# A two-block transformer step on one core: output projection, second norm and first queries ahead of the expert layer, in another order

## The chip, the cores and the metric

The kernel runs on one NeuronCore of a Trainium2 chip. The metric is the device time of one execution in microseconds, as the median of several runs; lower is better. PE (TensorE), ACT (ScalarE), DVE (VectorE) and POOL (GpSimd) each work through a queue of their own in a fixed order; SP issues the loads of weights and tables. Engines meet at semaphores only.

## The reference, cut to what matters

Two blocks are run one after the other. The first has two layers on 256 tokens `h` and 256 context tokens `hc`, width 1024; at the end of each layer:

```python
h = h + mod[:, 2] * mix                                   # mix = merged @ w_out
xn2 = modulate(rms_norm(h, norm2_g[l]), mod[:, 3], mod[:, 4])
h = h + mod[:, 5] * peer_ffn(xn2, peer_wq[l], peer_keys[l], peer_u[l], peer_v[l])
# peer_ffn, for each chunk of 128 tokens: q = xc @ w_q (8 heads x 2 halves x 128); scores of each half
# against 128 keys; the best 16 of each, the best 16 of their sums, softmax -> gates; for each of the
# 8 * 16 experts chosen: gelu(u_e . x) * gate * v_e, summed
```

All arithmetic is in float32. The second block (two layers of feed-forward, mixer and feed-forward) isn't touched by the change.

## The kernel before

Tokens are tiled in blocks of 128: blocks 0 and 1 are the tokens, 2 and 3 the context. The work is written out as one program for each engine (`tensor`, `scalar`, `vector`, `gpsimd`, `sync`, from line 2411 on), built of stages; each stage has a part for PE, ACT and DVE (`pe_...`, `act_...`, `dve_...`).

The expert layer is the long part. For each block 128 gathers run (one for each head and choice: 8 heads x 16), each of 1 MB: for each token the u and the v row of its expert (`pool_gather`, L2567), into a ring of up to ten slots. DVE forms u . x (L1718), ACT the gelu's tanh (L1147) and a diagonal of weights (L1132), and PE adds v through that diagonal (L699), which gives the slot back to POOL. The order of the gathers is fixed: stage A (layer 0) takes blocks 0, 1, 2, 3, stage C (layer 1) blocks 0, 1. `weave` puts other work between the steps of an expert stage in a fixed order: in A the routing of the other heads and blocks, the context's mixer and the next layer's start, in C the other heads' queries (`pe_rest`) and block 1's routing.

Routing turns queries into expert numbers, for two heads at a time (a head group): scores of the queries against the keys (PE, L675), copied by ACT (L1112), the best 16 and their pairs by DVE (`dve_route_pass`, L1609 to L1686), with an exponential by ACT (L1120). Block 0's first head group yields the indices of the first 32 gathers.

Ahead of each of the two expert stages stands a stretch with little beside it, written for both blocks at once. For T = "A" and T = "C" it runs:

- `pe_mixer_end`: the merged rows of both blocks are turned (L423; copied back by ACT L1075 and DVE L1574), then for each half n of the output columns the gate's rows (L423, copied by ACT L1081) and the product with w_out for both blocks (L430). DVE multiplies by the gate and adds to H (L1586, L1588), ACT takes the square sum (L921). A product of `gemm8` over 512 columns shows in the profile as 16 passes of 512 columns.
- the second norm, `pe_norm_turn`: one chain for both blocks (L1349, L1340, root L926, L1353), a diagonal for each block (L1359), then H is turned and scaled by PE (L456), with gain and shift by ACT (L939) and DVE (L1375), one half each.
- `pe_peer_rows`: the normed rows turned back for the experts (L423; copies L1095 and L1597).
- `pe_queries`: head group 0's queries, four products of eight matmuls over 256 columns, both blocks' tokens (L430; copies L1104 and L1606), which show as 64 passes.
- `pe_route_scores`: scores of block 0, group 0, followed by its routing.

`fence` makes ACT and DVE wait for all three engines; `edge` only marks how far each has come, for a later `after_edge`. Fences stand behind the mixer ("mixed A"), behind the attention of C ("attended D"), behind `mixer_end` ("ended") and behind the norm ("gather"); POOL starts the gathers after the mark "gather", and SP loads the keys after "ended A" and "attended D". SP's queue is in order: output weights (`("out", T, n)`), keys, then the query weights (`("wq", T, n)`, two loads of 1 MB for each head group) through a ring of four slots of 1 MB; a load waits until the slot's last reader is done.

## Time and profile before

| | us |
|---|---|
| median of 3 runs (4346.28 to 4356.92) | 4348.15 |
| profiled execution, first to last instruction (its own time: no other figure is given for it) | 4350.1 |
| PE busy | 3741.8 (86%) |
| DVE busy | 2841.1 (65%) |
| ACT busy | 1154.3 (27%) |
| POOL busy | 898.6 (21%) |
| first gather of stage A | 649.98 |
| first gather of stage C | 2575.40 |

The profile is that of one execution; times count from its first instruction. A matmul in float32 shows as two passes for each instruction. "L430" is line 430 of the kernel; an arrow in brackets names what ended the idle time in front of a row. PEld is the load of weights into PE, which lies beside the matmuls.

### The profile page before, as it was taken

What the parts mean: (1) busy time and instruction counts of PE and PEld (TensorE: products, weight loads), DVE (VectorE), ACT (ScalarE), POOL (GpSimd) and SP (SyncE); (2) the same over time, 40 slices, a digit from 0 to 9 for tenths busy, and PEclk for the clock granted to TensorE, in tenths of its full rate; (3) what the DMA queues carried; (4) which work ended last, traced back from release to release, by engine and by line L of the source; (5) the groups of instructions that cost most, each with busy time, mean ns of one, the idle gap of its engine ahead of it and who ended that gap; (6) DMA issues with size and microseconds to landing.
All of it is one profiled execution on the core that took longest, in us unless ns stands there. A gap on an engine that the chain in (4) does not pass through costs nothing. (4 is left out here: it accounts for less than half of the span.)

```text
span 4350.1 us, 42327 instructions
## 1 busy us (share of the span) xinstructions
PE 3741.8 (86%) x15261; PEld 2387.3 (55%) x15261; DVE 2841.1 (65%) x6605; ACT 1154.3 (27%) x2555; POOL 898.6 (21%) x772
## 2 busy tenths in 40 slices
PE   7999987878999867689896778777779989999898
PEld 3457554334755523245642545222229879898797
DVE  1342137897877788977876548886656576565765
ACT  2141011124111111231011411111124444444443
POOL 0000003433332334423331014543320000000000
PEclk7999998999999999999997889999999999999999
DMA  7273439998999999989996159999984534545443
GB/s 296 78 271 119 163 141 356 386 368 303 394 420 379 390 361 403 389 307 389 421 421 254 68 203 387 421 383 422 421 356 161 179 132 171 186 158 184 136 165 131
DMA packets 246623, 1225.90 MB, mean 282 GB/s; under 512 B 19257, under 2 KB 46203, under 8 KB 124429
## 3 DMA queue, kind: packets, MB, share of 16 engines
q0 software_dynamic: 110592, 805.36, 45.7%
q1 hardware_dynamic: 135820, 417.84, 26.0%
q8 instruction: 120, 1.97, 0.2%
q14 instruction: 91, 0.74, 0.0%
HBM read 1222.07 MB, written 1.05 MB: 281 GB/s over the span
## 5 line engine op out<-in xcount | busy, mean ns | idle before, releaser
L430 PE MATMUL ps<-wbuf,BIG 128*128 128x512 f32 x1856 | 813.3, 595 | 6.9 <-DMA wbuf<-in_t_conv_out_w 2.8
L2567 POOL DMA_INDIRECT gbuf<-in_t_uv,idx x286 | 341.3, 1193 | 1508.2 <-DVE BIG L1683 882.4
L430 PEld LDWEIGHTS ps<-wbuf,BIG 128*128 128x128 f32 x1856 | 352.7, 191 | 441.4 <-issue 433.3
L1759 DVE TENSOR_TENSOR plo<-wbuf,phi 128x1024 fp32r<-128x1024 f32 (+1 forms) x344 | 401.6, 1180 | 284.4 <-ACT phi L1167 283.7
L699 PE MATMUL ps<-gbuf,BIG 128*128 128x512 f32 x868 | 435.4, 641 | 165.8 <-ACT BIG L1132 165.4
L699 PE MATMUL ps<-BIG 128*128 128x512 f32 x904 | 438.2, 625 | 116.2 <-ACT BIG L1132 110.6
L1147 ACT ACTIVATE BIG<-BIG 128x2 f32<-128x2 f32 x384 | 78.1, 203 | 1430.9 <-DVE BIG L1725 1419.8
L724 PE MATMUL ps<-XH,phi 128*128 128x256 f32 x1472 | 422.0, 287 | 24.7 <-DVE XL L1769 20.8
L1718 DVE CUSTOM_DVE_ANT_0 BIG<-BIG 128x1024 f32<-128x1024 f32 x292 | 355.8, 1221 | 121.8 <-DMA BIG<-in_t_uv,idx 121.0
L430 PE MATMUL ps<-BIG,wbuf 128*128 128x256 f32 x1920 | 421.9, 380 | 0.3 <-DMA wbuf<-in_t_conv 0.2
L2567 POOL DMA_INDIRECT BIG<-in_t_uv,idx x292 | 337.6, 1156 | 406.5 <-PE ps L699 341.8
L1167 ACT CAST phi<-wbuf 128x1024 fp32r<-128x1024 f32 (+1 forms) x344 | 343.8, 1013 | 289.6 <-PE ps L726 289.1
L726 PE MATMUL ps<-XH,plo 128*128 128x256 f32 x1472 | 420.5, 286 | 0.0
L725 PE MATMUL ps<-XL,phi 128*128 128x256 f32 x1472 | 420.5, 286 | 0.0
L1718 DVE CUSTOM_DVE_ANT_0 gbuf<-gbuf,BIG 128x1024 f32<-128x1024 f32 x286 | 348.6, 1221 | 109.0 <-DMA gbuf<-in_t_uv,idx 108.6
L430 PEld LDWEIGHTS ps<-BIG,wbuf 128*128 128x128 f32 x1920 | 365.4, 191 | 64.7 <-issue 14.1
L699 PEld LDWEIGHTS ps<-gbuf,BIG 128*128 128x128 f32 x868 | 166.2, 202 | 409.6 <-ACT BIG L1132 231.5
L699 PE MATMUL ps<-wbuf,BIG 128*128 128x512 f32 x604 | 300.4, 627 | 94.2 <-ACT BIG L1132 94.0
L699 PEld LDWEIGHTS ps<-BIG 128*128 128x128 f32 x904 | 172.4, 198 | 363.6 <-issue 191.6
L2567 POOL DMA_INDIRECT wbuf<-in_t_uv,idx x190 | 219.5, 1155 | 417.0 <-PE ps L699 389.8
L724 PEld LDWEIGHTS ps<-XH,phi 128*128 128x128 f32 x1472 | 286.6, 195 | 26.7 <-DVE XL L1769 22.2
L1132 ACT ACTIVATE BIG<-ident,BIG 128x128 f32<-128x128 f32 x594 | 210.3, 395 | 298.3 <-DVE BIG L1701 276.8
(348 smaller groups left out, 5079.6 us busy)
## 6 DMA issues: line engine op xcount, KB each, us to landing
wbuf<-in_t_in SPq DMA_DIRECT2D x84, 1024.0 KB
wbuf<-in_t_w_mod SPq DMA_DIRECT2D x48, 1024.0 KB
wbuf<-in_ffn_wg SPq DMA_DIRECT2D x20, 2048.0 KB, 7.8
wbuf<-in_ffn_wu SPq DMA_DIRECT2D x20, 2048.0 KB, 7.8
wbuf<-in_t_conv SPq DMA_DIRECT2D x48, 768.0 KB
wbuf<-in_ffn_wd SPq DMA_DIRECT2D x16, 2048.0 KB, 8.0
wbuf<-in_t_peer_wq SPq DMA_DIRECT2D x24, 1024.0 KB
wbuf<-in_w_in SPq DMA_DIRECT2D x14, 1536.0 KB, 6.6
```

Source lines behind the costliest of these rows:

```text
L430: ins = p(mm)(bank, l, r, start=(k == 0), stop=(k == 7))
L699: ins = p(mm)(ps.of(("acc", T, tb, n)), dg, g[:, 1024 + n * 512:1536 + n * 512], start=(j == 0), stop=(j == last_on_pe(T, tb)))
L724: p(mm)(bank, lh, rh, start=(start and i == 0), stop=False)
L725: p(mm)(bank, lh, rl, start=False, stop=False)
L726: ins = p(mm)(bank, ll, rh, start=False, stop=(stop and i == n - 1))
L1132: a(act)(dg, ident[:, :], ACT.Copy, scale=wv[:, j:j + 1]).then_inc(act_exp.up(T, tb, "diag", j), 1)
L1147: a(act)(x2[:, j - 1:j + 1], x2[:, j - 1:j + 1], ACT.Tanh, scale=GELU_C * GELU_K).then_inc(act_exp.up(T, tb, "tanh", j // 2), 1)
L1167: a(copy)(piece_at(q)[0], W2.of(key, rows_, n)[:, k0:k1, c0:c1]).then_inc(act_piece.up(q), 1)
L1718: v(ttr)(row, row, XN[:, tb, :], 1.0, 0.0, ALU.mult, ALU.add, hid[:, j:j + 1]).then_inc(dve_exp.up(T, tb, "u", j), 1)
L1759: v(tt)(lo, W2.of(key, rows_, n)[:, k0:k1, c0:c1], hi.bitcast(F32), ALU.subtract).then_inc(dve_piece.up(q), 1)
L2567: g(nc.gpsimd.indirect_dma_start)(slot, None, I["t_uv"], bass.IndirectOffsetOnAxis(ap=idx[:, tb % 3, j:j + 1], axis=0)).then_inc(g_landed[ ...
```

## The change

For T = "A" and T = "C", the stages between the mixer (or attention) and the experts are replaced by one function for each engine, which takes the blocks one behind the other:

- PE's order is: block 0 turned, gate 0, product (n 0, block 0), gate 1, block 1 turned, products (1, 0) and (0, 1), norm of block 0, product (1, 1), rows of block 0, queries of block 0 (128 columns), its scores, then norm, rows and queries of block 1.
- The second norm has a chain for each block, so every instruction of that chain on DVE and ACT is issued twice, on one column in place of two. Queries are 128 passes of 128 columns in place of 64 of 256, with a copy for each block and product (eight in place of four).
- Block 0's halves are copied by ACT alone where the merged rows are turned; block 1's normed half, rows and queries are copied by ACT alone.
- The fences "ended" and "gather" become marks, in C also "attended D"; "mixed A" stays a fence.
- SP loads the keys behind the query weights of head group 0 instead of ahead of them; in A the mark "ended A" stands behind product (1, 1) and its square sum.
- Block 0's route pass on ACT copies the scores, does block 1's norm, rows and queries, and then its exponential.
- Context blocks ("B") are as before.

```diff
+        def pe_to_experts(p, T, l, L):
+            XT, MM = L.XT, L.MM
+            def merged_turn(tb):
+                for half in range(2):
+                    b = ps.claim(p, ("mt", T, tb, half), ((act_proj, dve_proj)[half * tb], (T, "mt", tb, half)))
+                    p.wait_ge(*(dve_att.at(T, tb, "merged") if T == "C" else dve_mix.at(T, "m", 1, 2, tb)))
+                    turn4(p, b, [MM[:, tb, k * 128:(k + 1) * 128] for k in range(half * 4, half * 4 + 4)]).then_inc(
+                        pe_proj.up(T, "mt", tb, half), 1)
+            def gate(n):
+                pe_gate_rows(p, ("og", T, n), l, 2, n, 0, act_proj, T, "gate", n).then_inc(pe_proj.up(T, "gate", n), 1)
+            def product(n, tb):
+                b = ps.claim(p, ("op", T, n, tb), (dve_proj, (T, "m", n, tb)))
+                p.wait_ge(*act_proj.at(T, "mt", tb, 0))
+                p.wait_ge(*(act_proj, dve_proj)[tb].at(T, "mt", tb, 1))
+                gemm8(p, b, ("out", T, n), 512, lambda k, w: (XT[:, k, tb * 128:(tb + 1) * 128], w)).then_inc(
+                    pe_proj.up(T, "op", n, tb), 1)
+                halves_done(("out", T, n), pe_proj, T, "op", n, tb)
+            def normed(tb):
+                N = second_norm(T, tb)
+                for half in range(2):
+                    b = ps.claim(p, ("norm", N, tb, half), ((act_norm, dve_norm)[half * (1 - tb)], (N, tb, "x")))
+                    p.wait_ge(*dve_norm.at(N, tb, "diag"))
+                    dg = diag_of(N, tb)
+                    for j in range(4):
+                        k = half * 4 + j
+                        ins = p(mm)(b[:, j * 128:(j + 1) * 128], H[:, tb, k * 128:(k + 1) * 128], dg, start=True, stop=True)
+                    ins.then_inc(pe_norm.up(N, tb, half), 1)
+            def rows_turned(tb):
+                N = second_norm(T, tb)
+                p.wait_ge(*act_norm.at(N, tb, "x"))
+                if tb == 0:
+                    p.wait_ge(*dve_norm.at(N, tb, "x"))
+                for half in range(2):
+                    b = ps.claim(p, ("xn", T, tb, half), ((act_peer, dve_peer)[half * (1 - tb)], (T, "xn", tb, half)))
+                    turn4(p, b, [XT[:, k, tb * 128:(tb + 1) * 128] for k in range(half * 4, half * 4 + 4)]).then_inc(
+                        pe_peer.up(T, "xn", tb, half), 1)
+            def queries(tb):
+                for j in range(4):
+                    b = ps.claim(p, ("pq", T, 0, j, tb), ((act_peer, dve_peer)[j % 2 * (1 - tb)], (T, "pq", 0, j, tb)))
+                    gemm8(p, b[:, 0:128], ("wq", T, 0), 512,
+                          lambda k, w: (w[:, j * 128:(j + 1) * 128], XT[:, k, tb * 128:(tb + 1) * 128])).then_inc(
+                              pe_peer.up(T, "pq", 0, j, tb), 1)
+                halves_done(("wq", T, 0), pe_peer, T, "pq", 0, 3, tb)
+            merged_turn(0)
+            gate(0)
+            product(0, 0)
+            gate(1)
+            merged_turn(1)
+            product(1, 0)
+            product(0, 1)
+            normed(0)
+            product(1, 1)
+            edge(p, "ended " + T)
+            rows_turned(0)
+            queries(0)
+            run(pe_route_scores(p, T, T, 0, 0, 2))
+            normed(1)
+            edge(p, "gather " + T)
+            rows_turned(1)
+            queries(1)
...
+        def act_to_experts(a, T, l, L):
+            XT = L.XT
+            def merged_turn(tb):
+                for half in range(2 - tb):
+                    a.wait_ge(*pe_proj.at(T, "mt", tb, half))
+                    a(copy)(XT[:, half * 4:half * 4 + 4, tb * 128:(tb + 1) * 128],
+                      ps.of(("mt", T, tb, half)).rearrange("p (j t) -> p j t", j=4)).then_inc(
+                          act_proj.up(T, "mt", tb, half), 1)
+            def gate(n):
+                g = tmp.enter(a, ("og", T, n))
+                a.wait_ge(*pe_proj.at(T, "gate", n))
+                a(copy)(g, ps.of(("og", T, n))).then_inc(act_proj.up(T, "gate", n), 1)
+            def squares(n, tb):
+                a.wait_ge(*dve_proj.at(T, "h", n, tb))
+                act_square_sum(a, T, tb, n, tmp.of(("om", T, n, tb)), norm_before(T))
+            def normed(tb):
+                N, scale, shift = second_norm(T, tb), colA(l, 1), colB(l, 1)
+                for half in range(1 + tb):
+                    b = ps.of(("norm", N, tb, half))
+                    a.wait_ge(*pe_norm.at(N, tb, half))
+                    for j in range(4):
+                        ins = a(act)(xt(L, half * 4 + j, tb), b[:, j * 128:(j + 1) * 128],
+                                ACT.Identity, bias=shift(half * 4 + j, tb), scale=scale(half * 4 + j, tb))
+                ins.then_inc(act_norm.up(N, tb, "x"), 1)
+            def rooted(tb):
+                N = second_norm(T, tb)
+                act_root(a, norm_row(N, (tb,)), dve_norm.at(N, "mean"), act_norm, N, "root")
+            def rows_copied(tb):
+                for half in range(1 + tb):
+                    a.wait_ge(*pe_peer.at(T, "xn", tb, half))
+                    a(copy)(XN[:, tb, half * 512:(half + 1) * 512], ps.of(("xn", T, tb, half))).then_inc(
+                        act_peer.up(T, "xn", tb, half), 1)
+            def queries(tb):
+                for j in range(0, 4, 2 - tb):
+                    a.wait_ge(*pe_peer.at(T, "pq", 0, j, tb))
+                    a(copy)(PQ[:, j, tb * 128:(tb + 1) * 128], ps.of(("pq", T, 0, j, tb))[:, 0:128]).then_inc(
+                        act_peer.up(T, "pq", 0, j, tb), 1)
+            merged_turn(0)
+            gate(0)
+            gate(1)
+            squares(0, 0)
+            merged_turn(1)
+            squares(1, 0)
+            rooted(0)
+            normed(0)
+            squares(0, 1)
+            squares(1, 1)
+            edge(a, "ended " + T)
+            rows_copied(0)
+            rooted(1)
+            queries(0)
+            route = act_route_pass(a, T, 0, route_before(T, 0, 0), 0, 2)
+            next(route)
+            normed(1)
+            edge(a, "gather " + T)
+            rows_copied(1)
+            queries(1)
+            run(route)
...
+        def dve_to_experts(v, T, l, L):
+            XT = L.XT
+            def summed(n, tb):
+                nn, g = slice(n * 512, (n + 1) * 512), tmp.of(("og", T, n))
+                m = tmp.claim(v, ("om", T, n, tb), (act_square, (T, tb, n)))
+                v.wait_ge(*pe_proj.at(T, "op", n, tb))
+                v.wait_ge(*act_proj.at(T, "gate", n))
+                v(tt)(m, ps.of(("op", T, n, tb)), g, ALU.mult).then_inc(dve_proj.up(T, "m", n, tb), 1)
+                v.wait_ge(*dve_proj.now())
+                v(tt)(H[:, tb, nn], H[:, tb, nn], m, ALU.add).then_inc(dve_proj.up(T, "h", n, tb), 1)
+            def norm_diagonal(tb):
+                N = second_norm(T, tb)
+                r = sts.claim(v, ("nm", N), (dve_norm, (N, tb, "diag")))[:, 0:1]
+                for n in range(2):
+                    v.wait_ge(*act_square.at(T, tb, n))
+                v(tt)(r, ssq[:, tb:tb + 1, 0], ssq[:, tb:tb + 1, 1], ALU.add).then_inc(dve_norm.up(N, "sum"), 1)
+                v.wait_ge(*dve_norm.now())
+                dve_mean(v, r, r, D, dve_norm, N, "mean")
+                v.wait_ge(*act_norm.at(N, "root"))
+                v(recip)(r, r).then_inc(dve_norm.up(), 1)
+                s = big.claim(v, ("dg", N, tb), (pe_norm, (N, tb, 1)))
+                v.wait_ge(*dve_norm.now())
+                v(ts)(s[:, 0:128], ident[:, :], r, None, ALU.mult).then_inc(dve_norm.up(N, tb, "diag"), 1)
+            for n in range(2):
+                tmp.take(("og", T, n), (dve_proj, (T, "m", n, 1)))
+            summed(0, 0)
+            v.wait_ge(*pe_proj.at(T, "mt", 1, 1))
+            v(vcopy)(XT[:, 4:8, 128:256], ps.of(("mt", T, 1, 1)).rearrange("p (j t) -> p j t", j=4)).then_inc(
+                dve_proj.up(T, "mt", 1, 1), 1)
+            summed(1, 0)
+            norm_diagonal(0)
+            summed(0, 1)
+            N, scale, shift = second_norm(T, 0), colA(l, 1), colB(l, 1)
+            v.wait_ge(*pe_norm.at(N, 0, 1))
+            for j in range(4):
+                ins = v(ts)(xt(L, 4 + j, 0), ps.of(("norm", N, 0, 1))[:, j * 128:(j + 1) * 128],
+                            scale(4 + j, 0), shift(4 + j, 0), ALU.mult, ALU.add)
+            ins.then_inc(dve_norm.up(N, 0, "x"), 1)
+            summed(1, 1)
+            edge(v, "ended " + T)
+            v.wait_ge(*pe_peer.at(T, "xn", 0, 1))
+            v(vcopy)(XN[:, 0, 512:1024], ps.of(("xn", T, 0, 1))).then_inc(dve_peer.up(T, "xn", 0, 1), 1)
+            norm_diagonal(1)
+            edge(v, "gather " + T)
+            for j in (1, 3):
+                v.wait_ge(*pe_peer.at(T, "pq", 0, j, 0))
+                v(vcopy)(PQ[:, j, 0:128], ps.of(("pq", T, 0, j, 0))[:, 0:128]).then_inc(dve_peer.up(T, "pq", 0, j, 0), 1)
+            run(dve_route_pass(v, T, l, 0, 0, 2))
...
-        def queries_in(p, T, K, n):
-            split = n == 0 and T != "B"
-            p.wait_ge(*act_peer.at(T, "pq", n, 2 if split else 3))
-            if split:
-                p.wait_ge(*dve_peer.at(T, "pq", n, 3))
+        def queries_in(p, T, K, tb, n):
+            if n or T == "B":
+                p.wait_ge(*act_peer.at(T, "pq", n, 3))
+            elif tb:
+                p.wait_ge(*act_peer.at(T, "pq", 0, 3, 1))
+            else:
+                p.wait_ge(*act_peer.at(T, "pq", 0, 2, 0))
...
-            run(pe_mixer_end(p, "A", 0, first))
-            edge(p, "ended A")
-            run(pe_norm_turn(p, "A2", range(2)))
-            edge(p, "gather A")
-            run(pe_peer_rows(p, "A", "A2", 0, first.XT, 0, 1))
-            run(pe_queries(p, "A", first.XT, range(1), 1))
-            run(pe_route_scores(p, "A", "A", 0, 0, 2))
+            pe_to_experts(p, "A", 0, first)
             weave(pe_experts(p, 0, AB, 0, 256), pe_context(p), 2)
...
-            fence(a, "attended D")
-            run(act_mixer_end(a, "C", 1, second, tmp))
-            fence(a, "ended C")
-            run(act_norm_turn(a, "C2", second, range(2), colA(1, 1), colB(1, 1)))
-            fence(a, "gather C")
-            run(act_peer_rows(a, "C", 0, 1))
-            run(act_queries(a, "C", range(1), 1))
-            run(act_route_pass(a, "C", 0, route_before("C", 0, 0), 0, 2))
+            edge(a, "attended D")
+            act_to_experts(a, "C", 1, second)
...
-            fence(v, "attended D")
+            edge(v, "attended D")
             tmp.reset()
-            run(dve_mixer_end(v, "C", 1, second, tmp))
-            fence(v, "ended C")
             big.reset()
-            run(dve_norm_turn(v, "C2", second, range(2), colA(1, 1), colB(1, 1), "C", big))
-            fence(v, "gather C")
-            run(dve_peer_rows(v, "C", 0, 1))
-            run(dve_queries(v, "C", range(1), 1))
-            run(dve_route_pass(v, "C", 1, 0, 0, 2))
+            dve_to_experts(v, "C", 1, second)
             weave(dve_experts(v, C, 0, 128), both(dve_rest(v, "C", 1), scaled(dve_route_pass(v, "C", 1, 1), 1.0, 1)), 2, BEHIND)
...
         def sync_peer(s, T, l):
-            if T != "B":
-                after_edge(s, {"A": "ended A", "C": "attended D"}[T])
-                load(s, ("keys", T), KY, I["t_keys"][l].rearrange("p (c k) -> p c k", c=16))
             for n in range(4):
                 two_halves(s, ("wq", T, n), I["t_peer_wq"][l, n])
+                if n == 0 and T != "B":
+                    after_edge(s, {"A": "ended A", "C": "attended D"}[T])
+                    load(s, ("keys", T), KY, I["t_keys"][l].rearrange("p (c k) -> p c k", c=16))
 ```

The call sites of ACT and DVE in A, and of PE in C, are changed in the same way.

## Rows read from the trace of the kernel before

**Rows 1.** Chain that ended last, 2530 to 2600: start us, us, what

```profile
2540.05 13.83 PE ps L430 x64
...
2554.59 1.14 PE ps L675 x8
...
2575.40 0.94 POOL gbuf L2567
```

**Rows 2.** Timeline, 565 to 650: start us, us, engine, line, operation, tiles, count, [idle before <-releaser]

```profile
569.95 0.69 DVE L1564 TENSOR_TENSOR BIG<-BIG,gbuf 128x512 f32<-128x512 f32 x1
...
570.81 1.17 ACT L1075 COPY BIG<-ps 128x512 f32<-128x512 f32 x2 [14.79 <-DVE BIG L1564]
...
572.78 13.97 PE L430 MATMUL ps<-wbuf,BIG 128*128 128x512 f32 x32 [0.55 <-DVE BIG L1574]
...
586.59 0.60 PE L423 MATMUL ps<-ident,modd 128*128 128x128 f32 x4
...
587.02 13.90 PE L430 MATMUL ps<-wbuf,BIG 128*128 128x512 f32 x32
...
602.41 0.63 ACT L921 ACTIVATE gbuf<-H 128x512 f32<-128x512 f32 x1 [6.14 <-DVE H L1588]
...
603.16 0.16 DVE L1349 TENSOR_TENSOR st<-ssq 128x2 f32<-128x2 f32 x1 [0.79 <-ACT gbuf L921]
...
603.63 1.28 ACT L926 ACT_TABLE_LOAD   x1 [0.50 <-DVE st L1340]
...
605.77 6.10 PE L456 MATMUL ps<-gbuf,H 128*128 128x128 f32 x32 [4.85 <-DVE gbuf L1359]
607.88 1.50 ACT L939 ACTIVATE BIG<-ps,modd,modA 128x128 f32<-128x128 f32 x4 [2.76 <-PE ps L456]
...
611.71 1.04 PE L423 MATMUL ps<-ident,BIG 128*128 128x128 f32 x8
...
614.32 13.98 PE L430 MATMUL ps<-BIG,wbuf 128*128 128x256 f32 x64
...
629.02 1.13 PE L675 MATMUL ps<-BIG 128*128 128x128 f32 x8 [0.72 <-DVE BIG L1606]
629.88 11.10 PEld L430 LDWEIGHTS ps<-BIG,wbuf 128*128 128x128 f32 x52
...
649.17 0.23 ACT L1120 ACTIVATE BIG<-BIG 128x32 f32<-128x32 f32 x1 [17.10 <-DVE BIG L1676]
...
649.98 1.08 POOL L2567 DMA_INDIRECT gbuf<-in_t_uv,idx  x1 [649.53 <-DVE BIG L1683]
```

**Rows 3.** Windows: us; busy us of each engine; TensorE clock granted, DMA share, GB/s

```profile
2486.00:2496.20 10.20, 2.65 (x25) 2.42 (x23) 6.49 (x7) 3.65 (x6) 0.00 (x0) 0.76 0.01 2
2498.90:2501.60 2.70, 2.70 (x4) 1.17 (x4) 0.00 (x0) 0.59 (x1) 0.00 (x0) 0.51 0.55 231
2522.00:2528.00 6.00, 6.00 (x15) 2.47 (x13) 0.95 (x2) 0.72 (x2) 0.00 (x0) 1.00 0.00 0
2590.00:2620.00 30.00, 24.78 (x57) 10.90 (x57) 27.86 (x100) 5.28 (x17) 12.18 (x12) 0.94 1.02 422
```

**Rows 4.** Timeline, 2482 to 2500

```profile
2487.61 1.04 PE L423 MATMUL ps<-ident,BIG 128*128 128x128 f32 x8
...
2490.66 0.21 ACT L926 ACTIVATE st<-st 128x8 f32<-128x8 f32 x1 [0.19 <-DVE st L1340]
...
2496.20 1.97 PE L423 MATMUL ps<-ident,BIG 128*128 128x128 f32 x8 [7.54 <-DVE BIG L2488]
```

**Rows 5.** Timeline of SP's queue, 2300 to 2800: start us, us until the last issue

```profile
2514.25 56.11 SPq L2579 DMA_DIRECT2D wbuf<-in_t_peer_wq  x8
```

**Rows 6.** DMA issues, 600 to 620: median us from issue to landing last

```profile
BIG<-in_t_keys SPq DMA_DIRECT2D x1, 1024.0 KB, 4.8
```

**Rows 7.** Timeline of PE, 2575 to 2680

```profile
2588.01 2.08 PE L675 MATMUL ps<-BIG 128*128 128x128 f32 x8 [18.47 <-ACT BIG L1104]
```

**Rows 8.** Timeline of POOL, 2570 to 2760

```profile
2640.52 0.95 POOL L2567 DMA_INDIRECT wbuf<-in_t_uv,idx  x1 [12.34 <-PE ps L699]
```

35 lines of the change are left out of this document (9 added, 26 removed).

## The prediction

> **What bounds the kernel now.** I read the chain of work that ended last first. Of the stretch ahead of the second expert stage it shows one file of single links: PE multiplies all queries of head group 0 for both token blocks (13.8 us), then the key scores, then DVE routes one block, then POOL issues the first gather at 2575.40 [rows 1]. Nothing runs in parallel on that path. So I read the timelines of the two such stretches, "A" (layer 0) and "C" (layer 1), and ask of each instruction whether the first gather needs it. In A [rows 2]: the second block's merged rows are turned, 570.81 to 572.78, then four products of the output projection, the norm of both blocks, the rows of both blocks, the queries of both blocks, and only at 629.02 the scores of block 0. From there it is 649.98 - 629.02 = 20.96 us to the first gather; in C 2575.40 - 2554.59 = 20.81 us [rows 1]. The gather that starts the stage needs block 0 alone. Behind that gather the stage is paced by transfers and slots: 422 GB/s and a DMA share of 1.02 between 2590 and 2620 [rows 3]. It starts when the first gather starts, so what the stretch ahead saves should come off the whole time.
>
> **The sum, counted to the start of block 0's scores.** Route, index and the start of the gather are untouched behind it.
>
> *Stretch A.* In the new order PE starts the first product when ACT has copied both halves of block 0. ACT is held by its fence until DVE's 569.95 + 0.69 = 570.64, starts at 570.81 as now, and two copies take 1.17 us: product at about 572.2 (now 572.78). Four products: the two pairs take 13.97 and 13.90, each with an end of some 0.15 that overlaps what follows, so 27.6. Between them now stand the gate's four turns (587.02 - 586.59, and a little: 0.5), block 1's eight (1.0) and block 0's norm products. The latter are 16 of the 32 passes which took 6.10 us with PE come from idleness, half of it slow; a pass of this shape at full clock takes about 0.12 us (eight turns take 1.04 us with their end), so 1.9 us. Then block 0's rows turned, 1.0; its queries, 64 passes of 128 columns; and the wait for DVE's last copy, 0.65 (614.32 + 13.98 to 629.02 is 0.72, with a shorter copy). [rows 2]
>
> **The price of a narrow query pass is not in the trace.** Now 64 passes of 256 columns take 13.98 us, 0.218 each. Bounds: half of that, 0.109, if columns set it, so 7.0 us; or 0.218 again, if the weight load sets it, so 14.0. The nearest row has the very shape, 128 by 128 with 128 columns out of the same tile: eight score passes start at 629.02 and the next weights begin 0.86 us later, so 0.111 a pass [rows 2]. I take 7.1 us. A page speaks against it: the Trainium skill, "Perfetto Trace Analysis", section "Optimizing Tensor Performance", holds larger matmuls more efficient than smaller ones. Taken at its hardest (no gain from half the columns) each stretch would give back 6.9 us; that is a rival below.
>
> Sum A: 572.2 + 27.6 + 0.5 + 1.0 + 1.9 + 1.0 + 7.1 + 0.65 = 611.95, against 629.02: **17.1 us** gained.
>
> *Stretch C.* The fence behind the attention becomes a mark, and block 0 was merged long ago. PE has nothing to do from 2487.61 + 1.04 = 2488.65 to 2496.20, while ACT and DVE finish block 1's attention norm. Now block 0's turns and the gate's come there, ACT copies behind its root (2490.66 + 0.21), so the first product starts at 2490.87 + 1.17 + 0.2 = 2492.25. The same 39.75 us follow (27.6 + 0.5 + 1.0 + 1.9 + 1.0 + 7.1 + 0.65). [rows 2, 4] PE's clock: it was at 0.76 on average between 2486 and 2496.2, so it fell some 5 us into that stretch, and after work began at 2496.20 it was still at 0.51 between 2498.9 and 2501.6 [rows 3]. The new gap, 2489.2 to 2492.25, may or may not let it fall. If it does, about 5.4 us run at 1.2 instead of 2.4 GHz, which costs 2.7; if not, nothing. I charge 2.7. Sum C: 2492.25 + 39.75 + 2.7 = 2534.7, against 2554.59: **19.9 us**; 22.6 without the cold start.
>
> **What I cost at nothing, and its cover.** (1) Block 0's norm chain: product (1,0) ends at about 587.5 in A; gate and add on DVE 1.5 (two of 0.69), square sum 0.75, then sum to diagonal 603.16 to 605.77 with the table load of 1.28, so 2.6: ready at 592.6, while PE is in product (0,1) until 594.4. Cover 1.8 us; without it PE would wait the rest. ACT's and DVE's halves of the normed block (1.5 each) lie under product (1,1), 6.9. (2) Block 1's norm, rows and queries: behind the scores on PE, under DVE's 18 us of routing. ACT must have done eight scalings (3.0), the row copies and four query copies before the exponential that now waits 17.10 us for DVE: block 1's queries end some 14 us behind the start of the scores, the exponential is due 20 behind it; cover 5 us. [rows 2] (3) The query weights of group 0 are loaded when product (0,1) is done, 594.4 in A. The load issued at 2514.25 had landed by 2522 at the latest, since nothing moved between 2522 and 2528 [rows 3, 5]; at most 7.7 us, so 602.1 against a need at 604.2. (4) The keys go to SP's queue behind these weights. In A they wait for the mark behind block 1's last square sum, 605.6, land 4.8 us later [rows 6] at 610.5, and are needed at 611.95: the thinnest cover, 1.5 us, with up to 3 us to lose. In C their mark is long past. SP stands behind that wait with group 1's weights (two loads), which are needed only at 626. (5) More weight loads on PE (64 in each stretch) lie in the passes' 0.111 us.
>
> **What moves behind the first gather.** Group 1's queries (64 more passes, 13.98 us) end now 15 us behind the start of the scores, six ahead of the first gather [rows 2], and free the slots for the last weights. In the new order PE does block 1's norm, rows and queries first; group 1's then end some 28 us behind the start of the scores, and the gather comes at 21. So they end 7 us behind it. PE has room: at the head of the stage it now idles 18.47 us for ACT's query copies, which stand behind the first tanh [rows 7], and some 5 us of that stay. But the last 2 MB of query weights come among the gathers: at 422 GB/s [rows 3] 5.0 us of transfer per stage. Bounds 0 (absorbed where POOL waits for a slot anyway, 12.34 us in one place [rows 8]) and 5.0; I take 2.5 each, the middle. The Trainium skill, "DMA: Bandwidth & Descriptors", section "Queues, rings and completion order", says that each transfer engine takes packets in turns from the queues with work, by which these weights would not wait behind the gathers but take their share at once; the sum by it is the upper bound, 5.0 per stage, 27.0 us gained. No row here separates it.
>
> Total: 17.1 + 19.9 - 5.0 = **32.0 us**. The profiled span is 4350.1, so 4318.1; the median of the runs stands 1.95 below the span, so I forecast **4316**.
>
> **The rivals.** *Forecast, 64 in 100*: own range 4305 to 4326 (37.0 + 2.7 + some luck; 27.0 less 3.0 for the keys in A and a little on the norm). *Narrow passes cost as wide ones, 7 in 100*: 14.0 in place of 7.1 in each stretch, 13.8 us less, gain 18, 4330. Against it stands the row with 0.111 us. *One expert stage gives its gain back, 16 in 100*: most likely A's, where four blocks of gathers are woven with a whole mixer and an earlier start meets other work; gain 15 to 20, 4331. Against: every queue follows the same fixed order. *More than the forecast, 6 in 100*: PE stays warm, the weights are absorbed, and the stage recycles slots better: 4300. *No effect, 4 in 100*: the change doesn't do what it says, because a late table load or copy in ACT's one file holds the scores; 4345. *Slower, 3 in 100*: in the stages PE frees gather slots in the order of its queue, and a run of woven products ahead of the freeing one stalls POOL, 12.34 us in one case [rows 8]. If the new phase makes such a meeting recur, each costs that. From three more on the 32 us are gone; four more give 4316 + 49 = 4365. Against it: the weave's order is the program's and stays.
>
> **How the numbers follow.** The range, 4302 to 4332, takes the forecast's own and most of the next three cases; what it leaves out is the 7 of no effect and slower, and the outer parts of the others, under 2 in 10. A measurement of this kernel can tell about 0.3%, 13 us, from no change. Faster by more: 64 + 7 + 16 + 6 = 93. Within: 4. Slower: 3.
>
> **What would show it.** Right: A's scores at 612 and its first gather at 633; C's 14.6 us ahead of the times above, since all behind A is shifted, so scores at 2520 and the first gather at 2541; 21 us between the two in both;  no idle time of PE between the four products and the queries beyond 1 us; query passes of 128 columns 0.11 us apart; 1908 us from A's first gather to C's, where it is 1925.4 now (less 19.9, plus 2.5). Wrong: scores waiting for the keys; a wait of PE for a diagonal or for weights; passes 0.2 us apart; or a distance from a stage's first gather to its end that grew by over 5 us.

## The result, and the profile after

| | before | after |
|---|---|---|
| median us of the first comparison (4 runs each) | 4349.92 | 4320.78 (4311.52 to 4322.23) |
| ratio, 95% interval | | 0.9920 [0.9908, 0.9932] |
| the same kernel in a later comparison (11 and 5 runs) | 4353.41 | 4319.55, ratio 0.9918 [0.9905, 0.9931] |
| profiled execution, span | 4350.1 | 4320.4 |
| PE busy | 3741.8 (86%) | 3740.2 (87%) |
| first gather of A / of C | 649.98 / 2575.40 | 629.92 / 2537.03 |

The kernel is faster by 29 to 34 us. PE does the same work (its busy sum differs by 1.6 us); what went is PE's idle time. Timeline of PE in the changed kernel in stretch A, which answers to [rows 2] (start us, us, engine, line, operation, tiles, count, idle before and its releaser):

```profile
566.68 1.04 PE L423 MATMUL ps<-ident,BIG 128*128 128x128 f32 x8
...
569.71 7.10 PE L430 MATMUL ps<-wbuf,BIG 128*128 128x512 f32 x16 [1.55 <-ACT BIG L1198]
...
577.96 13.90 PE L430 MATMUL ps<-wbuf,BIG 128*128 128x512 f32 x32
591.70 1.95 PE L711 MATMUL ps<-gbuf,H 128*128 128x128 f32 x16
593.48 7.03 PE L430 MATMUL ps<-wbuf,BIG 128*128 128x512 f32 x16
600.35 1.04 PE L423 MATMUL ps<-ident,BIG 128*128 128x128 f32 x8
601.22 7.31 PE L430 MATMUL ps<-BIG,wbuf 128*128 128x128 f32 x64
608.96 1.13 PE L675 MATMUL ps<-BIG 128*128 128x128 f32 x8 [0.43 <-issue]
609.93 1.95 PE L711 MATMUL ps<-gbuf,H 128*128 128x128 f32 x16
613.98 1.23 PE L423 MATMUL ps<-ident,BIG 128*128 128x128 f32 x8 [2.10 <-ACT BIG L1217]
615.01 22.65 PE L430 MATMUL ps<-BIG,wbuf 128*128 128x128 f32 x128
```

From the first product to the scores no row has an idle time in brackets but the 0.43 at their head. The 4.85 us in front of the norm's passes and the stop of 0.68 inside the row turns are gone, and the 0.72 in front of the scores is 0.43. Block 1's norm (609.93), rows and queries stand behind the scores; its queries run on into group 1's as one row of 128.

The same view of stretch C:

```profile
2472.03 0.60 PE L423 MATMUL ps<-ident,modd 128*128 128x128 f32 x4
2475.47 8.59 PE L430 MATMUL ps<-wbuf,BIG 128*128 128x512 f32 x16 [2.84 <-ACT BIG L1198]
...
2485.21 13.90 PE L430 MATMUL ps<-wbuf,BIG 128*128 128x512 f32 x32
...
2508.47 7.31 PE L430 MATMUL ps<-BIG,wbuf 128*128 128x128 f32 x64
2516.22 1.13 PE L675 MATMUL ps<-BIG 128*128 128x128 f32 x8 [0.43 <-issue]
...
2550.12 2.05 PE L675 MATMUL ps<-BIG 128*128 128x128 f32 x8 [6.83 <-ACT BIG L1173]
```

The first product comes 1.27 us behind the root of the attention norm at 2474.20; before, 8.33 behind it. It takes 8.59 us where A's takes 7.10: PE had been idle for 2.84 us, and the granted clock was 0.50 in the first 2.53 us of the product (windows in the last section). The last row is where PE waited 18.47 us before [rows 7]; it waits 6.83 now, since block 1's and group 1's queries fill PE up to 2543.29.

**Where the time came from, leg by leg.** Each leg is the difference of two starts in the same profile, before less after.

| leg | before | after | gained |
|---|---|---|---|
| start to block 0's merged rows being turned (A) | 568.95 | 566.68 | 2.27 |
| from there to A's first gather | 81.03 | 63.24 | 17.79 |
| A's first gather to C's root | 1840.68 | 1844.28 | -3.60 |
| C's root to C's first gather | 84.74 | 62.83 | 21.91 |
| C's first 16 gathers | 30.16 | 36.21 | -6.05 |
| 16th to last gather | 623.97 | 623.29 | 0.68 |
| last gather to the end | 1120.57 | 1123.87 | -3.30 |
| sum | | | 29.7 |

Three legs give back: A's stage, C's first gathers and the last leg. The last runs the same code in both kernels, and the experiments show its 3.30 to be scatter. The windows of C's first 16 gathers (us; busy us of PE, its weight loads, DVE, ACT and POOL; granted clock, DMA share, GB/s) show what fills the longer one. The kernel before:

```profile
2575.40:2605.56 30.16, 16.49 (x38) 8.04 (x39) 19.30 (x63) 5.14 (x17) 17.16 (x16) 0.70 0.98 401
```

The changed kernel:

```profile
2537.03:2573.24 36.21, 24.91 (x67) 13.76 (x67) 19.92 (x67) 5.17 (x18) 16.32 (x16) 0.81 0.96 391
```

The transfer engines are as full in both (0.98, 0.96), but 36.21 x 391 is 14.2 MB and 30.16 x 401 is 12.1 MB: 2.1 MB more came through. 2 MB is the size of group 3's query weights, which are now issued behind the first gather; whether they are the cause is tested below.

### The profile page after: what moved, and what is told of

Same layout as the page of the kernel before. It is cut to its first block, busy times and chain, and to the rows that moved or that the text cites. A ratio compares the mean times of both kernels' runs of the same rounds, so it can differ in the third digit from the quotient of the medians.

```text
span 4320.4 us, 42589 instructions
## 1 busy us (share of the span) xinstructions
PE 3740.2 (87%) x15389; PEld 2390.4 (55%) x15389; DVE 2834.3 (66%) x6599; ACT 1160.2 (27%) x2577; POOL 903.4 (21%) x772
## 4 chain that ended last, share of the span: by engine, by line
PE 39%; DMA 17%; DVE 16%; ACT 3%; issue 2%; POOL 1%; SPq 0%; DVEq 0%; ACTq 0%; POOLq 0%
PE ps L430 11%; DMA BIG<-in_t_uv,idx 10%; PE ps L793 7%; PE ps L794 7%; PE ps L795 7%; PE ps L768 5%; DMA gbuf<-in_t_uv,idx 4%; DVE BIG L1906 2%; DMA wbuf<-in_t_uv,idx 2%; DVE gbuf L1906 2%; DVE wbuf L1906 1%; PE ps L418 1%; DVE plo L1947 1%; DVE BIG L1899 1%; PE ps L423 1%
## 5 line engine op out<-in xcount | busy, mean ns | idle before, releaser
L430 PE MATMUL ps<-wbuf,BIG 128*128 128x512 f32 x1856 | 815.3, 596 | 15.3 <-DMA wbuf<-in_t_conv_out_w 6.6
L430 PEld LDWEIGHTS ps<-wbuf,BIG 128*128 128x128 f32 x1856 | 353.1, 192 | 448.9 <-issue 431.9
L430 PE MATMUL ps<-BIG,wbuf 128*128 128x256 f32 (+1 forms) x2048 | 425.4, 369 | 0.5 <-DMA wbuf<-in_t_conv 0.5
L430 PEld LDWEIGHTS ps<-BIG,wbuf 128*128 128x128 f32 x2048 | 373.0, 192 | 61.5 <-issue 14.6
## 6 DMA issues: line engine op xcount, KB each, us to landing
wbuf<-in_t_in SPq DMA_DIRECT2D x84, 1024.0 KB, 8.6
wbuf<-in_t_w_mod SPq DMA_DIRECT2D x48, 1024.0 KB, 7.4
wbuf<-in_t_peer_wq SPq DMA_DIRECT2D x24, 1024.0 KB, 7.1
```

What stands on the lines that cost most here:

```text
L430: ins = p(mm)(bank, l, r, start=(k == 0), stop=(k == 7))
```

## The experiments

What is counted in every run (us, from its profile; the root is the square root of C's attention norm; "first 16" and "first 32" run from the start of the first gather to that of the 17th or 33rd). In the kernels called sliver the last 2 MB of query weights of a stage are cut to 16 columns, 8 KB for each load; slot and early turn are two attempts at more. Each is explained in its place below.

| kernel | turns to gather A | first 32 gathers of A | gather A to root | root to gather C | first 16 of C | last gather to end |
|---|---|---|---|---|---|---|
| before | 81.03 | 95.14 | 1840.68 | 84.74 | 30.16 | 1120.57 |
| after | 63.24 | 98.59 | 1844.28 | 62.83 | 36.21 | 1123.87 |
| after again | 63.24 | 97.36 | 1845.12 | 62.85 | 35.80 | 1120.54 |
| only A | 63.25 | 97.53 | 1845.88 | 84.96 | 30.50 | 1120.59 |
| only C | 80.95 | 94.44 | 1843.60 | 62.92 | 35.12 | 1123.64 |
| keys first | 74.83 | 96.80 | 1844.71 | 63.04 | 35.21 | 1121.99 |
| fence D | 63.22 | 97.15 | 1841.47 | 69.00 | 35.00 | 1123.39 |
| route after | 74.69 | 94.84 | 1842.67 | 74.36 | 30.05 | 1123.10 |
| sliver, after | 63.24 | 92.96 | 1837.09 | 62.91 | 29.99 | 1123.60 |
| sliver, before | 81.23 | 94.85 | 1840.68 | 84.85 | 30.06 | 1127.67 |
| sliver, A only | 63.25 | 94.60 | 1840.70 | 62.86 | 37.38 | 1123.40 |
| slot | 63.24 | 97.20 | 1839.61 | 62.90 | 32.58 | 1126.73 |
| early turn | 63.23 | 97.83 | 1844.03 | 58.85 | 36.18 | 1123.29 |
| slot and turn | 63.24 | 97.49 | 1847.01 | 58.88 | 32.64 | 1123.16 |

In the two kernels with the early turn the root itself comes 0.8 us later behind its square than in the others. The two stretches repeat to 0.3 us, the first 16 gathers of C, with the same weights among them, to about 1 us but for one run (35.0 to 36.2; the 37.4 of "sliver, A only" isn't explained), the long legs only to 5 to 7 us. So a stretch can be read from one profile, the whole time can't.

**The new order in A alone.** `T == "C"` goes back to the old stages, fences and order of loads:

```diff
-            pe_to_experts(p, "C", 1, second)
+            run(pe_mixer_end(p, "C", 1, second)); edge(p, "ended C")
+            run(pe_norm_turn(p, "C2", range(2))); edge(p, "gather C")
+            run(pe_peer_rows(p, "C", "C2", 1, second.XT, 0, 1))
+            run(pe_queries(p, "C", second.XT, range(1), 1))
+            run(pe_route_scores(p, "C", "C", 0, 0, 2))
```
(and the same on ACT, DVE and SP)

> The token-block order stands in the stretch of layer 0 (A) alone; the one of layer 1 (C) is as before. My theory (each stretch shortens the path to its own first gather, A's expert stage keeps what it is given, C's gives 5 us back because the last 2 MB of query weights come among its gathers): A's first gather 17.8 us earlier than in the kernel before, C's first gather 84.7 us behind the square root that opens its stretch as before, no give-back behind it, so 17.8 less up to 2 of drift: 4350 - 17 = 4333, ratio 0.996. Rival 1 (A's expert stage gives the gain back, and all the gain is made in C): 4350, ratio 1.000. Rival 2 (the gain is all A's): 4321, ratio 0.9933.

Measured: 4335.86 against 4352.65, ratio 0.9963 [0.9951, 0.9975], so 16.8 us. Turns to gather 63.25, root to C's gather 84.96, no give-back in C's first 16 (30.50). The theory had 4333 and holds; both rivals fall.

**The new order in C alone.** The same edit for "A".

> The token-block order stands in layer 1 (C) alone; A is as before. My theory: the first gather of C comes 62.8 us behind the root that opens the stretch (84.7 before), 21.9 us gained, of which 5.0 to 6.0 are given back within the first 16 gathers, where 2 MB of query weights come in between; whole time 4350 - 16.4 = 4333.5, ratio 0.9962. Rival 1 (the give-back in C comes from what A's earlier start did to the stages between): no give-back here, 4328, ratio 0.995. Rival 2 (C's gain is lost in its expert stage): 4348 or more, ratio 0.9995.

Measured: 4334.13, ratio 0.9960 [0.9946, 0.9974], 18.5 us. Root to gather 62.92, first 16 gathers 35.12: the give-back is there with A unchanged, so it isn't made by A's earlier start. The two halves make 35.3 us together, the whole 29 to 34; within the intervals they add up.

**The keys ahead of group 0's weights again.**

```diff
             for n in range(4):
-                two_halves(s, ("wq", T, n), I["t_peer_wq"][l, n])
                 if n == 0 and T != "B":
                     after_edge(s, {"A": "ended A", "C": "attended D"}[T])
                     load(s, ("keys", T), KY, ...)
+                two_halves(s, ("wq", T, n), I["t_peer_wq"][l, n])
```

> The changed kernel, with the keys ahead of the query weights of group 0 in SP's queue again. In A both then wait for the mark behind the last square sum, at 602.8, and 3 MB land behind it: at the 422 GB/s of the profile 7.5 us of transfer and some 2.3 until it lands, so about 612.6; block 0's queries, which started at 601.2, then start about 11 us later. In C the keys' mark is long past, no loss. My theory: 10.5 us lost in A's stretch, first gather of A at about 640.5 instead of 629.9; 4321 + 10.5 = 4331.5. Rival 1 (the order of these loads is covered by the products, as it was before): 4321. Rival 2 (the delay is absorbed by the expert stage of A behind it): first gather late by 10, whole time 4322 to 4325.

Measured: 4333.37, ratio 0.9959 [0.9944, 0.9974], some 13 us above the changed kernel's 4320.78 of the first comparison. PE in stretch A of this kernel:

```profile
595.67 1.04 PE L423 MATMUL ps<-ident,BIG 128*128 128x128 f32 x8
605.62 2.08 PE L430 MATMUL ps<-BIG,wbuf 128*128 128x128 f32 x8 [8.91 <-DMA wbuf<-in_t_peer_wq]
608.10 7.34 PE L430 MATMUL ps<-BIG,wbuf 128*128 128x128 f32 x56 [0.41 <-DMA wbuf<-in_t_peer_wq]
615.88 1.13 PE L675 MATMUL ps<-BIG 128*128 128x128 f32 x8 [0.43 <-issue]
```

Here a wait for the mark held the whole queue of SP: keys and weights were issued together at 598.12, and PE stood 8.91 us for the first half. Turns to gather grew by 11.6 (10.5 expected), and nothing behind absorbed it. Without the swap of the two loads, two thirds of A's gain are gone. In C, where the mark is long past, the order costs nothing: root to gather is 63.04.

**The fence behind C's attention put back.**

```diff
-            edge(a, "attended D")
+            fence(a, "attended D")
-            edge(v, "attended D")
+            fence(v, "attended D")
```

> The changed kernel with the fences of ACT and DVE behind the attention of layer 1 put back (the mark becomes a wait again). Block 0's turned rows can then be copied only when block 1 has been merged too, 5.5 us behind the root. My theory: the first product of C starts 7 us behind the root (1.3 in the changed kernel), 5.5 us lost, and up to 1 more by a colder TensorE; C's first gather 68.5 us behind the root (62.8); 4321 + 5.5 = 4326.5. Rival 1 (ACT and DVE were late anyway, the fence costs nothing): 4321. Rival 2 (most of C's gain hangs on this fence, PE's products cannot run ahead): 10 us or more, 4331.

Measured: 4326.33, ratio 0.9945 [0.9930, 0.9960]. Timeline of PE in C:

```profile
2478.41 9.31 PE L430 MATMUL ps<-wbuf,BIG 128*128 128x512 f32 x16 [8.30 <-ACT BIG L1198]
```

The first product stands 6.7 us behind the root (2471.68), and costs 9.31 instead of 8.59. Root to gather 69.00 against 62.83: 6.2 us hang on this fence, of which 0.7 on the colder TensorE.

**Block 1's norm, rows and queries ahead of block 0's scores.**

```diff
             queries(0)
-            run(pe_route_scores(p, T, T, 0, 0, 2))
             normed(1)
             edge(p, "gather " + T)
             rows_turned(1)
             queries(1)
+            run(pe_route_scores(p, T, T, 0, 0, 2))
```

> The changed kernel with block 1's norm, rows and queries of group 0 put ahead of block 0's key scores on PE and ACT, in both stretches. My theory: in the changed kernel they take PE from 609.93 to 622.3 behind the scores; ahead of them they delay the scores by that, 12.5 to 13.4 us a stretch (A's scores 49 to 50 us behind the last turns of block 0's merged rows' start + 3, about 622 on the changed kernel's clock). Group 1's queries then end 6 us ahead of the first gather again, so C's first 16 gathers take 30 us (36 in the changed kernel) and 5 us come back. Whole time 4321 + 26 - 5 = 4342. Rival 1 (only the order of the products and norms of block 0 brought the gain, this part nothing): 4321. Rival 2 (weights behind the first gather are not what C's first 16 gathers pay for): they still take 35 or more, whole time 4347.

Measured: 4339.04, ratio 0.9967 [0.9954, 0.9980]. Turns to gather 74.69, root to gather 74.36: 11.5 us in each stretch, where I had expected 12.5 to 13.4. PE in A of this kernel:

```profile
597.25 7.31 PE L430 MATMUL ps<-BIG,wbuf 128*128 128x128 f32 x64
604.39 1.95 PE L711 MATMUL ps<-gbuf,H 128*128 128x128 f32 x16
608.45 1.09 PE L423 MATMUL ps<-ident,BIG 128*128 128x128 f32 x8 [2.10 <-ACT BIG L1217]
609.38 7.31 PE L430 MATMUL ps<-BIG,wbuf 128*128 128x128 f32 x64
616.52 1.06 PE L675 MATMUL ps<-BIG 128*128 128x128 f32 x8
```

From 604.39 to 616.52 PE does block 1's work, 12.13 us; the head of the scores loses its 0.43 in turn. And C's first 16 gathers take 30.05 again: with block 1's queries done early, the last weights are issued at 2548.60, 5.8 us ahead of the first gather (2554.43). So routing first gains 23 us in the stretches and gives some of it back through those weights. Such losses do not add up to the gain: in A, taking back the loads' order alone costs 11.6 and taking back this order alone 11.5, 23.1 together, where the whole change gains 17.8. Each says what is lost without that part, not a share.

**The last 2 MB cut away, in the changed kernel and in the one before.** Group 3's queries are computed from stale weights in both.

```diff
-                two_halves(s, ("wq", T, n), I["t_peer_wq"][l, n])
+                two_halves(s, ("wq", T, n), I["t_peer_wq"][l, n], 16 if n == 3 and T != "B" else None)
-                tile(s, key + (h,), src[h])
+                tile(s, key + (h,), src[h][:, 0:cut] if cut else src[h])
```

> The changed kernel, of which the last 2 MB of query weights (group 3) of A and of C are cut to 16 columns, so group 3's queries are computed from stale weights. My theory (these 2 MB are what C's stage gives back, and A's stage absorbs them): C's first 16 gathers take 30.2 us instead of 35 to 36, A's 32nd gather comes 3.5 us earlier but its last at the same time; whole time 4321 - 5 = 4316. Rival 1 (both stages pay, as my 2.5 each had it): 4311 to 4316, with A's last gather 2.5 to 5 earlier too. Rival 2 (the give-back is POOL's or PE's, e.g. slots freed late because PE does group 1's queries behind the first gather): C's first 16 gathers still take 35, 4321.

> The kernel before, with the same 2 MB cut to 16 columns in A and C. My theory: they had landed ahead of the first gather, so nothing changes: C's first 16 gathers take 30.2 us as before, ratio 1.000 (within 0.0005). Rival (any 2 MB less in the stage are worth their transfer time, wherever they lie): 5 us faster in C and up to 5 in A, ratio 0.998 to 0.9985.

Measured: the changed kernel without them 4309.4, ratio 0.9903 [0.9889, 0.9918]; the kernel before without them 4356.72 against 4355.16, ratio 1.0001 [0.9990, 1.0013]. C's first 16 gathers take 29.99 and 30.06. PE's and POOL's order is that of the changed kernel, so rival 2 of the first expectation falls. In the kernel before, these weights were issued at 2569.56, 5.8 us ahead of the first gather, and 2.1 MB had moved by 2576.5, 1.1 us behind it; there the load is worth nothing. In C of the changed kernel it is issued 6.3 us behind the first gather and is worth 6.2 us (5.6 by the means over all runs). My theory's other half, that A's stage absorbs its share, isn't borne out by this run: from A's first gather to the root it took 1837.09, 7.2 less than the changed kernel. Hence the cut in A alone, further down. The issues of transfers from 2537 to 2550 in the changed kernel (the last number is the median us from issue to landing):

```profile
wbuf<-in_t_peer_wq SPq DMA_DIRECT2D x2, 1024.0 KB, 11.8
BIG<-in_t_uv,idx POOLq DMA_INDIRECT x5, 20.3
gbuf<-in_t_uv,idx POOLq DMA_INDIRECT x3, 8.2
wbuf<-in_t_uv,idx POOLq DMA_INDIRECT x2, 15.6
```

The same of the first gathers in the kernel with the sliver:

```profile
BIG<-in_t_uv,idx POOLq DMA_INDIRECT x5, 14.5
gbuf<-in_t_uv,idx POOLq DMA_INDIRECT x3, 7.6
wbuf<-in_t_uv,idx POOLq DMA_INDIRECT x2, 10.8
```

The 11.8 is the middle of two loads: the first, issued at 2543.32, landed 9.5 us later at 2552.8, the second, issued at 2543.69, 14.1 us later at 2557.8. The gathers issued at 2540.75 and 2541.99 landed at 2555.1 and 2558.8. So the first MB overtook both, the second MB only the later one, while gathers issued in the same microseconds took 20.3. The loads do not stand behind all gathers issued before them, but they are slowed: where no gather runs, two such loads took 4.9 and 7.0 us (591.89 and 592.26), and even the cut ones of 8 KB took 7.1 and 9.3 us here. The gathers into BIG became 5.8 us slower by the 2 MB. That agrees with the Trainium skill, "DMA: Bandwidth & Descriptors", section "Queues, rings and completion order", which has each transfer engine take its queues in turn.

**The same cut in A alone**, to see what A's stage pays (`T == "A"` in the line above).

> The changed kernel with group 3's query weights (2 MB) cut to 16 columns in A alone; with them cut in both stretches the first 32 gathers of A took 93.0 us (97 to 98.6 in the new order with them, 94.4 to 95.1 in the old), and the way from A's first gather to C's root 1837.1 (1839.6 to 1845.9 otherwise). Theory 1 (A's stage pays for them as C's does): first 32 gathers 93, first gather to C's root 1837 to 1838, whole time 5 to 6 below the changed kernel's in the same comparison. Theory 2 (A's stage absorbs them, the 1837.1 was its scatter): first 32 gathers 93, but first gather to C's root 1840 to 1845, whole time equal within 2.

Measured: 4319.60, ratio 0.9914 [0.9899, 0.9928], beside 4319.55 of the changed kernel. First 32 gathers of A 94.60 (96.8 to 98.6 with the weights behind the gather), gather to root 1840.70. At its head A's stage does pay, about 3 us; whether it keeps that debt up to C isn't settled. Gather to root is 1839.6 to 1847.0 in the eight kernels that carry the weights behind A's gather (mean 1844.0), 1840.7 to 1843.6 in the three where they come ahead of it (1842.3), and 1837.1 and 1840.7 in the two changed kernels without them (1838.9). Between behind and ahead it is 2 us, between behind and without 5, and the eight kernels of the first group, with the same code in A's stage, already differ by 7. The two whole times decide nothing at this size.

**First attempt at more: one of the two megabytes put elsewhere in C.**

```diff
+                    if T == "C":
+                        W.where[("wq", T, 3, 0)] = 4
+                        s(nc.sync.dma_start)(W.slots[4], I["t_peer_wq"][l, 3, 0]).then_inc(W.coming(("wq", T, 3, 0)), 16)
```
(W gets a fifth slot, H[:, 2:4, :], which is left out of its turns; the line stands behind the load of the keys)

> An attempt to keep more of the gain: the changed kernel, where in C the first half (1 MB) of group 3's query weights goes to the rows of the context, which nothing reads any more, and is loaded right behind the keys, some 30 us ahead of the first gather. My theory: 1 MB less among C's first gathers, 2.5 us at 422 GB/s: the first 16 take 33 instead of 35 to 36, whole time 4318.5, ratio to the kernel before 0.0006 lower than the changed kernel's. Rival 1 (the give-back is not these weights): 4321. Rival 2 (the 1 MB ahead delays the query weights of group 0 or 1, since it stands before them in the queue): C's first gather later by up to 2.5, 4321 or more.

Measured: 4315.56, ratio 0.9912 [0.9898, 0.9926]. Window of C's first 16 gathers:

```profile
2534.69:2567.27 32.58, 22.29 (x67) 12.74 (x67) 19.24 (x63) 5.14 (x17) 16.60 (x17) 0.90 0.96 392
```

32.58 x 392 is 12.8 MB, 1.4 less than the changed kernel's. 36.21, 32.58, 29.99 us for 2, 1 and 0 MB behind the first gather: the give-back grows with the bytes, 2.6 us for the first MB and 3.2 to 3.6 for the second (by the mean of 35.8 or by this pair). Root to gather is 62.90, so the load put ahead delays nothing.

**Second attempt: ACT copies block 0's turned rows ahead of the root.**

```diff
                     yield 2
+                    if early and qb == qbs[-1]:
+                        early()
                     act_root(a, attn_row(T, qb), dve_att.at(T, qb, "mean"), act_att, T, qb, "root")
```
(`early` is the copy of block 0's turned rows, taken out of act_to_experts for C)

> An attempt to save more in C: the changed kernel, where ACT copies block 0's turned rows right behind the square sum of the attention norm instead of behind the root that follows it. PE has them ready at 2472.0 on the changed kernel's clock, the copies would end at 2473.9 instead of 2475.4, and block 1's root comes 1 us later, which product (0,1) covers. My theory: first product 2.3 us behind the start of that square (3.8 in the changed kernel), 1.5 us gained, and with PE idle for 1.3 instead of 2.8 us its granted clock stays up, so the first product pair takes 7.1 instead of 8.6: 3.0 in all, first gather of C 62.4 us behind the square (65.4). Rival 1 (the clock falls all the same, it had begun to before): 1.5, first gather 63.9. Rival 2 (block 1's later merge delays product (0,1)): 0 to 1 gained. Whole time 3 lower than the changed kernel's, which is below what one comparison can tell.

Measured: 4321.63, ratio 0.9925 [0.9912, 0.9938]. PE in C:

```profile
2474.38 7.11 PE L430 MATMUL ps<-wbuf,BIG 128*128 128x512 f32 x16 [1.14 <-ACT BIG L1197]
```

First product 2.12 us behind the start of the square (2472.26), first gather 62.19 behind it (62.4 forecast, 65.38 in the changed kernel): 3.2 us. Rival 1 falls: the 16 passes took 7.11. The whole time doesn't show the gain, nor could it.

**Both attempts.**

> Both attempts together (1 MB of group 3's weights in the context's rows, early copy of block 0's turned rows in C). My theory: they add up, 2.6 + 3.0 = 5.6 us below the changed kernel in the same comparison, 4315; C's first gather 62.4 us behind the square and its first 16 gathers 32.6. Rival (the load put ahead takes the bandwidth that group 0's weights need, now that the queries start 3 us earlier): first gather 65 or more behind the square, gain 2.6.

Measured: 4316.33, ratio 0.9906 [0.9891, 0.9922], with 4319.55 for the changed kernel beside it. The legs add up as forecast: 62.21 behind the square, 32.64 for the first 16 gathers, so some 6 us from the two legs. The medians show 3.2, and the intervals overlap: by the legs this is the best version, by the whole time it isn't shown to be faster than the changed kernel. It is faster than the kernel before.

**The changed kernel once more.**

> The changed kernel once more, in the same comparison as the three others. 4321, ratio 0.992 to 0.993; A's first gather 63.2 us behind the start of block 0's turns, C's 62.9 behind its root, first 32 gathers of A 97 to 98.6, first 16 of C 35 to 36.2; from A's first gather to C's root 1840 to 1846, from the last gather to the end 1121 to 1127, which is how much two executions of one code differ here.

Measured: 4319.55, ratio 0.9918 [0.9905, 0.9931]. Its legs stand in the table; the last leg is 1120.54 here and 1123.87 in the first profile of the same code, and 1120.57 and 1127.67 with the code of before (the second with the weights cut, which this leg doesn't use). So the 3.30 us that this leg seemed to cost are scatter.

## Why the prediction was right, and where its terms were off

**The mechanism and the sum.** The forecast of 4316 was 32.0 us below the kernel before in one profile; the runs gave 29 and 34. The three terms, against what was measured:

| term | predicted | measured |
|---|---|---|
| stretch A | 17.1 | 17.8 |
| stretch C | 19.9 | 21.9 |
| weights behind the gather, C | -2.5 | -5.6 (35.8 against 30.2, the means of the seven kernels with 2 MB behind the gather and of the four with them ahead) |
| weights behind the gather, A | -2.5 | -2 to -5, open |

The mechanism is as forecast. That the sum came so close is partly luck, because its errors cancel: C's gain was put 2.0 too low and its give-back 3.1 too low.

**Stretch A.** The product started 3.03 us behind the turns (3.25 taken), the passes took what the sum said within 0.3, and the wait in front of the scores was 0.43, not 0.65. The price on which most hung, a pass of 128 columns, is 0.112: in the kernel with block 1's part ahead of the scores, the 64 passes at 597.25 are followed by the next at 604.39. I had taken 0.111 from eight score passes [rows 2]. The rival of narrow passes that cost as wide ones falls, and with it the hard reading of the Trainium skill, "Perfetto Trace Analysis", section "Optimizing Tensor Performance": in this shape half the columns cost half the time.

**Stretch C.** Root to scores was to be 44.0 and is 42.0. Of the 2.0, 1.2 is the cold start: I charged 2.7, for 5.4 us at half clock as in [rows 3], and it cost 1.5 (8.59 - 7.10), for the clock was back 3 us behind the product's start. The product started 1.27 behind the root (1.59 taken), 0.3; the wait for DVE gave 0.2; the remaining 0.3 lies in the chain of passes.

**The covers.** (1) Norm chain: the diagonal was ready at 589.24 (DVE's 588.95 + 0.29), PE wanted it at 591.70, cover 2.5 (1.8 predicted). (2) Block 1 under the routing: ACT's last query copy began at 623.88, and after the table load ACT still waited 3.66 us for DVE before the exponential; cover held. (3) Group 0's weights: the halves were issued at 591.89 and 592.26 and landed 4.9 and 7.0 later, at 596.8 and 599.3; the queries start at 601.22; cover at least 2.0 (2.1 predicted). (4) Keys: issued at 602.81, landed 4.9 later at 607.7, needed at 608.96; cover 1.3, the thinnest, as forecast. Rows of ACT and DVE in the changed kernel on which these rest:

```profile
587.22 1.28 ACT L995 ACT_TABLE_LOAD   x1
...
588.95 0.29 DVE L1851 TENSOR_SCALAR gbuf<-ident,st 128x128 f32<-128x128 f32 x1
...
602.00 0.63 ACT L990 ACTIVATE gbuf<-H 128x512 f32<-128x512 f32 x1 [7.10 <-DVE H L1837]
...
623.88 0.27 ACT L1234 COPY BIG<-ps 128x128 f32<-128x128 f32 x1 [1.52 <-PE ps L430]
624.17 1.28 ACT L1189 ACT_TABLE_LOAD   x1
629.11 0.23 ACT L1189 ACTIVATE BIG<-BIG 128x32 f32<-128x32 f32 x1 [3.66 <-DVE BIG L1812]
```

The table load at 587.22 lies ahead of the root here; in [rows 2] it is in the chain too, so it is no new cost. SP's queue:

```profile
591.89 0.81 SPq L2734 DMA_DIRECT2D wbuf<-in_t_peer_wq  x2
602.81 0.33 SPq L2729 DMA_DIRECT2D BIG<-in_t_keys  x1
603.18 35.34 SPq L2734 DMA_DIRECT2D wbuf<-in_t_peer_wq  x6
```

**What moved behind the first gather: the term that was mis-sized.** That group 1's queries would end 7 us behind the gather was right (7.7 in A, 6.3 in C). The step that failed is the choice of the middle between the bounds 0 and 5.0, 2.5 for each stage: in C it measured 5.6, beyond the upper bound. The row I had for absorption was one stall of POOL 65 us into the stage [rows 8]. At the head of the stage nothing is left to absorb: POOL issues ten gathers at once (2537.03 to 2548.79), and between 2547 and 2573 the transfer engines are full. In the changed kernel:

```profile
2547.00:2552.00 5.00, 1.88 (x9) 1.91 (x10) 2.56 (x8) 1.86 (x7) 2.21 (x2) 0.50 1.02 429
2552.00:2557.00 5.00, 4.36 (x9) 1.58 (x8) 1.72 (x5) 0.79 (x2) 1.30 (x2) 0.84 1.00 421
2557.00:2562.00 5.00, 3.70 (x8) 1.44 (x8) 3.00 (x9) 0.69 (x2) 1.83 (x3) 1.00 1.01 423
```

So a byte more there costs at least its time at the 422 GB/s of [rows 3]. Nothing shows that C's stage wins it back: from 2573.24 to its last gathers the transfer engines' share is 0.99, and the 16th to the last gather take 624.2 us on average in the seven kernels with the 2 MB behind the first gather and 624.5 in the five without, with 622.3 to 626.9 from run to run. The upper bound, to which the Trainium skill, "DMA: Bandwidth & Descriptors", section "Queues, rings and completion order", had led, was the nearest value. That 5.6 is more than the 5.0 of transfer is not explained by any run.

**The signs I named.** The scores came at 608.96 and 2516.22 where I had said 612 and 2520, the first gathers at 629.92 and 2537.03 (633 and 2541); 2.27 us of each is that this execution reached the stretch earlier, which has nothing to do with the change (that start lies between 561.5 and 572.6 in the fourteen profiles). 21 us from scores to gather: 20.96 and 20.81, unchanged. 1908 us from gather to gather: 1907.11, though by errors that cancel in part. No wait for keys, weights or the diagonal. One sign that I had named for being wrong did come up: from C's first gather to its last it was to grow by no more than 5 us, and it grew by 5.37 (654.13 to 659.50). It is the same mis-sized term. **The rivals:** one stage giving its gain back falls for the greater part with the two halves of the change run alone (A's stage may still give back 2 to 5 us); POOL stalls that recur would have lengthened the 16th to the last gather in the changed order, and it is the same within its scatter.

## What to carry to other kernels

Where a stage behind is paced by transfers, ask two things of a reorder: which single block does its first transfer need, and which loads slide from ahead of that first transfer to behind it. The first gave its full time here; the second cost at least bytes over bandwidth in C, where the stage had no idle transfer time at that very place. And when a load moves past another in an in-order queue, check what each waits for: here a swap of two loads was worth 11.6 us in A, because one of them waited for a mark, and nothing in C, where the mark was long past.

## What the hardware showed that I had not expected

- **A short idle time decides the clock.** In C's stretch PE stood 2.84 us for ACT and then ran at half clock; with 1.14 us, in the kernel with the early copy, it did not. This holds in every profile with C's new order and without the fence: in the eight with 2.84 us of idle time the 16 passes took 8.59 to 8.80, in the two with 1.14 they took 7.11. Windows from PE's first product on, in the changed kernel:

```profile
2475.47:2478.00 2.53, 2.53 (x3) 1.15 (x4) 2.46 (x3) 0.39 (x1) 0.00 (x0) 0.50 0.00 0
2478.00:2481.00 3.00, 3.00 (x8) 1.39 (x7) 1.65 (x2) 0.00 (x0) 0.00 (x0) 0.92 0.00 0
```

and in the kernel with the early copy:

```profile
2474.40:2477.00 2.60, 2.60 (x6) 1.20 (x7) 1.48 (x4) 1.87 (x3) 0.00 (x0) 1.00 0.00 0
2477.00:2480.00 3.00, 3.00 (x8) 1.33 (x7) 2.90 (x4) 0.00 (x0) 0.00 (x0) 1.00 0.00 0
```

0.50 is 1.2 GHz, 1.00 is 2.4. Behind 8.30 us of idle time, with the fence put back, the same passes took 9.31. So 1.7 us less of waiting brought 3.2.

- **A direct load can overtake gathers that were issued before it, at their cost.** Of 2 MB issued at 2543.32 and 2543.69, the first MB landed at 2552.8, ahead of the gathers issued at 2540.75 and 2541.99, and the second at 2557.8, between them; the gathers into BIG issued around them took 20.3 us instead of 14.5.

- **Equal code, unequal legs.** From the last gather to the end, one code took 1120.54 and 1123.87, another 1120.57 and 1127.67. A profile's whole span says nothing on a change of 3 us; the legs of the changed stretches, which repeat to 0.3 us, can show it.
